# Products of no use where TensorE waits, in the first part of the mixers stages of a two-layer backbone step

## What is computed

```python
def _trunk_layer(x, mod, lp, gla_s0, rw_s0, grid):
    sh1, sc1, gt1, sh2, sc2, gt2, sh3, sc3, gt3 = [mod[:, j, None, :] for j in range(N_MOD)]
    h = _rmsnorm(x, lp['ffn1_norm']) * (1.0 + sc1) + sh1
    x = x + 0.5 * gt1 * _swiglu(h, lp['ffn1_w_in'], lp['ffn1_w_out'])
    h = _rmsnorm(x, lp['mix_norm']) * (1.0 + sc2) + sh2
    m, s_gla, s_rw = _token_mix(h, lp, gla_s0, rw_s0, grid)
    x = x + gt2 * m
    h = _rmsnorm(x, lp['ffn2_norm']) * (1.0 + sc3) + sh3
    x = x + 0.5 * gt3 * _swiglu(h, lp['ffn2_w_in'], lp['ffn2_w_out'])

def _token_mix(h, lp, gla_s0, rw_s0, grid):
    p = (h @ lp['mix_w_in']).astype(jnp.float32)
    p_gla, p_hy, p_rw = _split(p, [GLA_COLS, HY_COLS, RW_COLS])
    o_gla, s_gla = _gla_mixer(p_gla, lp, gla_s0)    # 6 heads, chunks of 64, both directions
    o_hy = _hyena_mixer(p_hy, lp)                   # long convolution by FFT
    o_rw, s_rw = _rwkv_mixer(p_rw, lp, rw_s0, grid) # 6 heads of 64, both directions
    o = jnp.concatenate([o_gla, o_hy, o_rw], axis=-1).astype(h.dtype)
    return o @ lp['mix_w_out'], s_gla, s_rw
```

## Time and profile before

| | us |
|---|---|
| three timed runs | 1964.58, 1965.21 (median), 1968.77 |
| the profiled execution | 1964.49 |
| its span, from the first to the last instruction | 1962.7 |
| TensorE busy | 1888.3 (96%) |
| mean granted TensorE clock | 0.984 of full |
| `mixers_stage` of layer 0 | 476.3 to 694 |
| `mixers_stage` of layer 1 | 1429.5 to 1638 |

### The profile page before, as it was taken

The page is one execution under the profiler, slowest core; times in us unless marked ns, Lnnn a source line. Parts: engine busy times, 40 slices in busy tenths (PEclk is TensorE's granted clock), DMA queues, the critical chain, the costliest instruction groups (busy, mean ns, idle before and its releaser), DMA issues. The chain is left out here.

```text
span 1962.7 us, 38653 instructions
## 1 busy us (share of the span) xinstructions
PE 1888.3 (96%) x16410; PEld 1734.6 (88%) x16410; DVE 1092.8 (56%) x1853; ACT 740.4 (38%) x1113; POOL 31.6 (2%) x64
## 2 busy tenths in 40 slices
PE   5999999999899999999999999999979899999998
PEld 2988999897566889999999999999947698999997
DVE  3544444776666475554445554467656756655533
ACT  3333333435353153333343333344443425433322
POOL 0000000000010000000000000000010100000000
PEclk9999999999899999999999999999979999999999
DMA  7766334422555443333343333352241304333332
GB/s 278 274 219 216 117 119 138 177 86 83 181 159 156 131 150 129 124 114 114 121 160 118 120 126 105 131 180 106 86 134 49 90 25 154 129 124 114 107 132 91
DMA packets 73335, 263.25 MB, mean 134 GB/s; under 512 B 9712, under 2 KB 11120, under 8 KB 57072
## 3 DMA queue, kind: packets, MB, share of 16 engines
q1 hardware_dynamic: 73200, 261.27, 39.3%
HBM read 259.08 MB, written 2.16 MB: 133 GB/s over the span
## 5 line engine op out<-in xcount | busy, mean ns | idle before, releaser
L160 PE MATMUL ps<-h_head,w_head 128*128 128x386 f32 x1824 | 624.6, 343 | 4.2 <-ACT h_head L293 2.1
L160 PE MATMUL ps<-h_head,w_rest 128*128 128x386 f32 x1824 | 619.8, 340 | 0.0
L160 PE MATMUL ps<-h_rest,w_head 128*128 128x386 f32 x1824 | 617.9, 339 | 0.0
L223 ACT ACTIVATE w_head<-w_raw 128x2048 fp32r<-128x2048 f32 (+1 forms) x176 | 303.0, 1722 | 595.4 <-PE ps L160 579.0
L226 DVE TENSOR_TENSOR w_rest<-w_raw,w_head 128x2048 fp32r<-128x2048 f32 (+1 forms) x176 | 360.7, 2049 | 223.2 <-ACT w_head L223 223.2
L160 PEld LDWEIGHTS ps<-h_head,w_head 128*128 128x128 f32 x1824 | 346.4, 190 | 26.4 <-issue 19.8
L160 PEld LDWEIGHTS ps<-h_head,w_rest 128*128 128x128 f32 x1824 | 346.4, 190 | 0.0
L160 PEld LDWEIGHTS ps<-h_rest,w_head 128*128 128x128 f32 x1824 | 343.1, 188 | 0.2
L160 PE MATMUL ps<-gu_head,w_head 128*128 128x384 f32 x832 | 278.7, 335 | 0.1
L160 PE MATMUL ps<-gu_head,w_rest 128*128 128x384 f32 x832 | 278.0, 335 | 0.0
L160 PE MATMUL ps<-gu_rest,w_head 128*128 128x384 f32 x832 | 278.0, 335 | 0.0
(11 more groups left out here) (297 smaller groups left out, 1777.7 us busy)
## 6 DMA issues: line engine op xcount, KB each, us to landing
w_raw<-in_w_in SPq DMA_DIRECT2D x88, 1024.0 KB, 4.9
w_raw<-in_ada_w SPq DMA_DIRECT2D x48, 1024.0 KB, 6.2
w_raw<-in_w_out SPq DMA_DIRECT2D x64, 704.0 KB, 4.0
w_raw<-in_mix_in SPq DMA_DIRECT2D x26, 1024.0 KB, 4.9
ada_raw<-in_ada_w SPq DMA_DIRECT2D x24, 1024.0 KB, 6.2
w_raw<-in_mix_out SPq DMA_DIRECT2D x8, 1024.0 KB, 4.8
hyena_const<-in_hconst SPq DMA_DIRECT2D x2, 1792.0 KB, 9.2
x<-in_x_in SPq DMA_DIRECT2D x1, 1536.0 KB, 11.9
```

The costliest lines, as they stand in the source:

```text
L160: return nc.tensor.matmul(out, lhsT, rhs, start=start, stop=stop)
L223: return nc.scalar.activation(self.HI[src], self.RAW[src], ACT.Copy)
```

## The change

A helper `keep_busy(pe, b, n)` issues n products of the identity with itself into PSUM bank b. Fifteen lines call it in the two lists, 47 products in layer 0 and 57 in layer 1. Where they go to bank 6, which holds the gate and then the bonus of pair A, `after_shared` first waits for those to be taken out. Nothing is removed or moved.

```diff
+                def keep_busy(pe, b, n):
+                    for _ in range(n):
+                        mm(bank(b, 128), cst("ident"), cst("ident"))
+
+                def after_shared(pe):
+                    A.after_act(pe, "g")
+                    A.after_dve(pe, "bon")
...
                     if sets == 4:
+                        keep_busy(pe, 0, 6)
                         ada(pe, 0, 0)
...
                         ada(pe, 0, 3)
+                        after_shared(pe)
+                        keep_busy(pe, 6, 3)
                         A.pe_gram(pe, 0, 1)
+                        keep_busy(pe, 6, 10)
                         A.pe_gram(pe, 0, 2)
```

More of the change, by code:

```diff
@@ L2511, in _ @@
                         ada(pe, 0, 1)
+                        keep_busy(pe, 0, 5)
                         A.pe_nat(pe, 0)
@@ L2519, in _ @@
                         ada(pe, 0, 3)
+                        after_shared(pe)
+                        keep_busy(pe, 6, 3)
                         A.pe_gram(pe, 0, 1)
+                        keep_busy(pe, 6, 10)
                         A.pe_gram(pe, 0, 2)
                         ada(pe, 0, 4)
+                        keep_busy(pe, 6, 14)
                         ada(pe, 0, 5)
+                        keep_busy(pe, 6, 3)
                         A.pe_gram(pe, 1, 0)
+                        keep_busy(pe, 6, 6)
                         G.pe_turn_k(pe, 0)
@@ L2743, in _ @@
                         ada(pe, 0, 2)
+                        after_shared(pe)
+                        keep_busy(pe, 6, 4)
                         A.pe_gram(pe, 0, 0)
+                        keep_busy(pe, 6, 10)
                         A.pe_gram(pe, 0, 1)
                         ada(pe, 0, 3)
+                        keep_busy(pe, 6, 8)
                         A.pe_gram(pe, 0, 2)
+                        keep_busy(pe, 6, 4)
                         ada(pe, 0, 4)
+                        keep_busy(pe, 6, 14)
                         A.pe_gram(pe, 1, 0)
+                        keep_busy(pe, 6, 6)
                         G.pe_turn_k(pe, 0)
```

## The result

The changed kernel takes **1971.3 us** (median of 12 runs, 1965.1 to 1980.8), the kernel before beside it 1965.5 us (12 runs); the ratio is **1.0033 [1.0020, 1.0045]**. In a second comparison it was 1.0021 [1.0007, 1.0035]. Predicted were 1956 us and a gain of 9.3 us; it is a loss of 4 to 6 us. The profiled execution took 1967.81 us, with a span of 1965.9. Single executions of one program lie up to 21 us apart here, so small differences are read from the ratios, and single profiles only for what they show at a place.

What follows compares the result with a forecast made beforehand. TensorE's unbroken last stream follows the mixers stages, slowed by half clock; -3.0 us in layer 0 and -6.3 in layer 1 make -9.3 from 1964.49, so 1955.2, stated as 1956 for the median; range 1950 to 1966.

Steps and rivals of the forecast that it cites:

- What bounds the kernel: Last 313.39 us are unbroken TensorE work from the second mixers stage's end, so moving a stage's end moves the kernel's end.
- The four stretches at half clock: Two in each layer's mixers stage, 41.2 us together, where the clock and not a wait makes busy TensorE slow.
- The price of a product: Each added product is two records of 0.12 us, so 0.24 us at full clock; 0.48 us at half clock.
- The begin: Start of the mixers stage: full clock brings DVE's second taking to 484.5 in layer 0 (1.0 us gained), 1437.0 in layer 1.
- the first rival: The first clock fall at the stage's begin stays, the six products coming after the idleness; 1958 us, chance 0.15.
- The middle: First gram product to `G.pe_update` (layer 0) or `G.pe_scores` (layer 1): products hold full clock, gaining 2.0 and 5.6 us.
- The price of the cover: Layer 0, after the 14 products: an `ada` unit starts 1.9 us later than it could, keys wait until 506.3 for turning.
- the shift should hold to the end of each stage: Behind the changed places the same instructions follow in order at the same clock, keeping -3.0 and -6.3 us.
- The second rival: Clock falls where it fell before, around 501.8 and 1457.6, and the products run at half clock; 1974 us, chance 0.13.
- The third: Clock falls behind the last added products, where only narrow work follows, about 5.5 us in each layer; 1966 us, chance 0.12.
- The fourth: More is won: later clock falls at 590.60 and 1553.14 may vanish, some 5 us, or multiply; 1950 us, chance 0.08.

Runs made afterwards that it cites:

- the narrow ones: Changed kernel with the same number of added products, each 8 columns wide instead of 128; 2004.0 us, ratio to the kernel before 1.0172.
- the fitted and aligned kernels: Changed kernel cut to 22 and 27 products where TensorE idled, later instructions moved by whole packets; ratio 0.9974, again 0.9959; without the begin's six 1.0002.
- the kernel with layer 0 aligned: Changed kernel cut to 22 and 27 products, instructions behind layer 0's products moved a whole packet, layer 1's left off packet places; 1961.6 us, ratio 0.9960.
- the full counts: Changed kernel with all 104 products, filled up with added instructions to whole packets; 1970.4 us, ratio to the kernel before 1.0013.
- the fitted ones: Changed kernel with products only where TensorE idled, 22 in layer 0 and 27 in layer 1; without whole packets 1972.3 us, ratio 1.0010.

## Why the prediction was wrong, step by step

- **What bounds the kernel: right.** (The four stretches at half clock add up to 40.95 us, not 41.2.) The last stream is the same length to 0.01 us, and whatever moves the ends of the mixers stages moves the end.
- **The price of a product: right.** 28 records took 3.39 us, 20 took 2.50 us: 0.12 us a record. At half clock the narrow ones give 0.22 us, at the floor that I took (0.24).
- **The begin: right where the clock held.** 484.48 for the second taking against 484.5 predicted, without a wait, though 0.25 us of that come from the stage's earlier begin; in layer 1 1441.53, less the 4.47 us of the later begin 1437.06, against 1437.0. But it holds only sometimes. Over the profiles of all kernels but the narrow one, the clock fell at the begin of 18 of 18 stages without the six products, and of 13 of 20 with them (for 3.4 or 10.2 us). So the first rival (15%) was the more frequent case, and the same program does both. Its price of 2.9 us no run isolates; with and without the six, the fitted and aligned kernels differ by 5 to 7 us in the median.
- **The middle: the clock right, the work in it mis-sized.** No profile with all the middle products has a fall there. But I had twelve transposes at 1.35 us, from nine of one size; they took 2.7 us (507.01 to 509.74) in layer 0 and 2.5 in layer 1, since each pair of a large and a small one takes 0.46 us. The trace of the kernel before had told it: there the twelve took from 505.14 to 509.32, 4.18 us at half clock (the line below stands behind them), and half of that is 2.1. With the first gram product, which came 0.45 us later than put, that is 1.8 of the 2.1 us by which layer 0's first part fell short. In layer 1 the first gram product came no earlier (1450.03, less the 4.47 us of the stage's later begin, against 1445.51) where I had 0.7, and with the transposes that is 1.9 of the 2.2 us. The price of the cover was in the text: 1.9 us at one `ada` unit, and in layer 0 keys that are ready at about 504.2 and wait until 506.3, 2.1 us, where 2.2 were measured. For layer 1, where they waited 2.75 us, it was not.

```profile
509.32 1.94 PE L160 MATMUL ps<-w_raw,cond_silu 128*32 128x512 f32 x8
```

- **The step that failed: "the shift should hold to the end of each stage".** It rested on the same instructions in the same order. They are not in the same place, and not always at the same clock. Layer 0's stage loses 5.3 us behind `G.pe_update`: 3.8 by pauses in which TensorE waits for a packet of instructions (7.2 us against 3.4), 1.4 at the block's end, and 1.2 by a new fall of the clock right behind a pause, less about 1.5 that a shorter fall gave back. Moving the stream alone by 64, 128 or 188 places costs 0.5%, by 256 nothing. None of the rivals had this; the pauses stood in the trace of the kernel before (0.97, 1.00, 1.42 and 1.46 us, released by nothing), and I had not asked what they were.
- **The second rival (the products at half clock)** is not what made the loss: its place is the middle, and the clock held there. **The third** is not seen in the changed kernel: clock 1.00 through the turning and the update in both layers. The Trainium skill ("TensorE: Matmul & The Clock Gate", Part 4: PE-mode transpose) says that transposes do not count as busy for the clock in the way products do. Profiles with fewer products agree better with it: in the kernel with layer 0 aligned the clock fell for 3.4 us behind the last transposes of either layer, which start at 1461.31 and 512.35 (the windows shown with that kernel). No run isolates it. **The fourth** came in the sense of its last sentence, "they may as well multiply": the fall at 590 us is half as long and the one at 1553 us is gone, but there are three others (672.16, 1528.90 and 1545.97), 13.6 us in all against 10.2.

The sum: predicted -9.3 in the profiled execution, found +3.2. Of the 12.5 us between, 4.3 are the two first parts, 5.3 the rest of layer 0's stage, and 2.8 the rest of layer 1's. There the pause at 1478.10 added 1.0 us and falls of the clock at 1528.90 and 1545.97 1.3 and 1.1, while the fall at 1553.14 and the pause at 1615.15 are gone, 1.4 and 1.5 us; the rest is in steps below 1 us that I did not follow. With the place restored and the counts fitted, the gain is 5 to 8 us by the ratio, against 9.3 predicted for twice the products and a clock that never falls.

What stays open: why three different shifts cost the same 0.5%, though their pauses differ, and why the clock stood longer at 0.50 in them; why the alignment won only 0.1 to 0.2% for the full counts but 0.4 to 0.5% for the fitted ones; and why a packet comes late at one border and not at the next. That the kernel before stands at a lucky place is only argued: it was better than three places of three.

## What to carry to other kernels

Before you believe that untouched code behind your edit will run as before, look in the trace for waits that nothing releases, and make a control that moves the code by as many instructions, without the edit. Where it costs, fill up to whole packets of instructions, and judge the edit there. Products that keep the clock up need only fill the idle time: half as many held it as well, and each more stands in front of the step that everybody waits for.

## What the runs showed of the hardware

- TensorE pauses of 0.2 to 2.8 us that no semaphore explains, among short products (24 of 64x64 in 0.92 us), at borders of 256 instructions (16 KB, one packet of its instruction queue). All 87 of 0.5 us or more end 1.20 to 1.59 us after a packet has landed.
- A product with full weights costs 0.12 us a record at full clock with 8 columns as with 128 (2.40 and 2.50 us for 20).
- An instruction of two satisfied waits costs TensorE's sequencer 106 ns, and where nothing hides it, it delays what is behind it: 64 of them ahead of the first product, which waited for a DMA, moved that from 7.92 to 8.21 us, 130 to 15.30.
- Half clock costs less than half of its length here: over the 147 executions of the kernel before, 1 us more of it goes with 0.19 us more time (51 to 107 us at 0.50), and in the fitted and aligned kernels 27 to 33 us less went with 5 to 8 us less.
